# Routed experts in an alternating order, four table marks in flight, down remainders one item later, and the last rows prepared sooner

## The chip, the cores and the metric

The kernel runs on one core of one Trainium2 chip. The metric is the device time of one execution in microseconds (us). TensorE multiplies matrices; VectorE, ScalarE and GpSimd work on rows; SyncE issues most of the transfers, and GpSimd the gathers, the scattered additions and the accumulating loads.

## The reference

One encoder layer on 1024 tokens of width 1024, in fp32:

```
xn  = rms_norm(x);  z = xn @ w_in
A   = spatial gating of gelu(z[:, :1024]);  B = real part of a 2-D DFT of z[:, 1024:]
h   = x + concat(rms_norm(A), rms_norm(B)) @ w_out
hn  = rms_norm(h)
eidx, gates = top 8 of 64 experts for each token (sigmoid scores, best 4 of 8 groups)
routed[t]  = sum over the 8: gates * (silu(hn @ w_gate[e]) * (hn @ w_up[e])) @ w_down[e]
out = rms_norm(h + routed + shared expert)
```

An expert has a hidden width of 256. Its tokens are padded to a multiple of 128. The order in which the experts are done changes nothing but the rounding of sums.

## The kernel before, in words

The first part (projection, gating, DFT, w_out, router scores; lines 322 to 638) is not touched. Each token's expert set lies in `mask`.

**Routing tables** (lines 1249 to 1321 on VectorE, 667 to 703 on TensorE). TensorE counts the tokens of each expert by a product with ones. VectorE turns counts into numbers of 128-row pieces (`nch`), TensorE makes their running sum over the experts (line 686), VectorE derives from it `cols`: for item number p the expert (row 0 of `tab`) and twice the expert plus a bit for "first item of its expert" (row 1). Line 690 turns `cols` into rows, line 1296 writes `tab`, from which all engines read their registers (`look`). Then, chunk by chunk of 128 tokens, VectorE makes `mark` and `pick` (lines 1304, 1306) and TensorE multiplies them (`table`, line 663); the sum in `ps[5]` becomes `idx_all` and `row_all`, the token rows of every item. `mark` and `pick` have two places each, so chunk c waits for the product of chunk c - 2. Between these steps TensorE computes the shared expert (`s_gate_up`, `s_down`), and VectorE its `shared_h`.

**Items.** An item is 128 rows of one expert. Items come in turns of three (`TURN`), and a loop runs over the turns; the first and the last turn are written out. The experts are taken in the order of their numbers. An expert with more than 128 tokens has two items. For item i:
- GpSimd gathers its rows, three items ahead (`gather`), keeps the gate column (`keep_gate`, line 1527), and adds the result rows into DRAM (`add_rows`, line 1543), into one of two copies of y.
- TensorE runs, per step: the transposes of item i+1 (`turn_item`, line 460), `down(i - 1)` (line 733), `turn_h(i)` (line 741), `gate_up(i + 1)` (line 719). Every fp32 product is made of three in a faster format: high by high, high by rest, rest by high.
- ScalarE runs silu(i), `evac_xT(i + 1)`, the high half of the gate weights of item i+2 if that item starts an expert (`split_gu`, line 944), `evac_h(i)`, `evac_out(i - 1)`, the high half of the up weights, and then `split_dn` of item i+1's expert (line 948).
- VectorE runs `gated_h(i)` (hh, line 1329), `rest_xT(i + 1)` (xTl, 1336), the remainder of the gate weights for item i+2 (`rest_gu` part 0, line 1188), `rest_h(i)` (hTl, 1341), part 1, and `rest_dn` of item i+1's expert (1195).
- SyncE loads gate and up weights (1 MB each, lines 284 and 285) and down weights (1 MB, line 288) into two places each. A load waits until both halves of the expert two before are made (`load_next_gu`, `load_next_dn`).

TensorE's `down(i)` waits for the down weights (`s_hd`, `s_ld`) and for hTl (`s_hl`), and `gate_up(i)` for its weights (`s_hg`, `s_lg`) and xTl (`s_xd`).

**The end.** The rows of the last three items are not added in DRAM: GpSimd makes three one-hot matrices (`onehot`, line 1593), TensorE multiplies them with the last results (`last_rows`, 771), and VectorE adds the product to y (`add_last`, 1417). y is loaded by SyncE (line 448), and the second copy by accumulating loads of GpSimd (line 1601). `onehot` lies in `raw_dn`'s memory, so GpSimd and SyncE wait for the last `rest_dn` (lines 439 to 442 and 1587 to 1590).

The parts of VectorE's item that the change moves:

```
rest_xT(i + 1)
with dv.If(ahead[0] > 0): rest_gu(ahead[2], ahead[1], (0,))
rest_h(i)
with dv.If(ahead[0] > 0): rest_gu(ahead[2], ahead[1], (1,))
with dv.If(coming[0] > 0): rest_dn(coming[2], coming[1])
```

## Time and profile before

| | us |
|---|---|
| median of 3 runs | 1400.49 (1398.68 to 1400.86) |
| the profiled execution | 1402.79 |
| its span in the trace | 1401.1 |
| TensorE busy | 1327.6 (95%) |
| VectorE busy | 860.0 (61%) |
| ScalarE busy | 726.3 (52%) |
| GpSimd busy | 477.6 (34%) |
| HBM, mean over the span | 253 GB/s |

Times in rows are us from the start of the span. A row of the order of time has start, duration, engine, line, operation, written and read tiles, and in brackets the idle time of its engine before it and what ended that. Lines are those of the kernel before.

### The profile page before, as it was taken

Reading aid. Unit: us, or ns where it says so; the run is one execution under the profiler, and the core shown is the slowest. Engines: PE = TensorE matmul, PEld = TensorE weight load, DVE = VectorE, ACT = ScalarE, POOL = GpSimd, SP = SyncE. Lnnn points to the kernel's source line nnn. Section 1 sums busy time; section 2 is a strip of 40 time slices with the busy share of each in tenths; the row PEclk is TensorE's granted clock in tenths of the full one; section 3 lists DMA queues with packets and bytes.
Section 4 is the critical chain, followed back from the end, with each engine's and each line's share of the span. In section 5 each row is a group of like instructions: output and inputs, shape, how many; then the busy total and the mean of one; then the engine's idle time right before and its main releaser. Section 6 shows DMA issues by size and latency. Waiting matters only on the chain.

```text
span 1401.1 us, 25069 instructions
## 1 busy us (share of the span) xinstructions
PE 1327.6 (95%) x6025; PEld 1036.9 (74%) x6026; DVE 860.0 (61%) x1186; ACT 726.3 (52%) x916; POOL 477.6 (34%) x610
## 2 busy tenths in 40 slices
PE   6999988999999999999999999999999999999995
PEld 5885465888445888888878888878877788788774
DVE  5430543446565667667866566786687756675665
ACT  5321244221011576756865557675577756665752
POOL 2431201000001345435543334453354433433462
PEclk9999998999999999999999999999999999999998
DMA  9604022102306799999998889999899998998979
GB/s 347 181 6 161 5 115 91 46 31 102 131 16 233 251 307 329 341 294 317 336 369 264 247 264 297 375 351 276 262 350 372 354 268 264 323 317 273 301 240 242
DMA packets 88306, 338.01 MB, mean 241 GB/s; under 512 B 12497, under 2 KB 23761, under 8 KB 71505
## 3 DMA queue, kind: packets, MB, share of 16 engines
q1 hardware_dynamic: 60624, 250.53, 46.0%
q0 software_dynamic: 27648, 87.06, 27.5%
q8 instruction: 18, 0.29, 0.1%
q14 instruction: 16, 0.12, 0.0%
HBM read 288.99 MB, written 65.27 MB: 253 GB/s over the span
## 4 chain that ended last, share of the span: by engine, by line
PE 73%; DMA 9%; ACT 6%; DVE 4%; issue 4%; ACTq 2%; DVEq 1%; SPq 0%; POOL 0%; POOLq 0%
PE ps L719 28%; PE ps_out L733 11%; PE ps L611 6%; PE ps L477 6%; DMA raw_gu<-in_w_up 5%; PE ps L460 5%; PE ps L646 4%; PE ps L513 4%; ACT w_gu L944 3%; DMA ya_in<-y_rows_dram 2%; PE ps L562 2%; ACT w_dn L948 2%; DVE xTl L1336 1%; DMA raw_dn<-in_w_down 1%; PE ps_out L628 1%
## 5 line engine op out<-in xcount | busy, mean ns | idle before, releaser
L719 PE MATMUL ps<-w_gu,xTh 128*128 x1488 | 473.2, 399 | 21.6 <-DVE xTl L1336 20.6
L1188 DVE TENSOR_TENSOR w_gu<-raw_gu,w_gu (+1 forms) x128 | 293.5, 2293 | 106.8 <-ACT w_gu L944 106.3
L719 PEld LDWEIGHTS ps<-w_gu,xTh 128*128 128x128 f32 x1488 | 276.6, 190 | 84.6 <-issue 29.3
L719 PE MATMUL ps<-w_gu,xTl 128*128 x744 | 293.6, 395 | 0.0
L944 ACT ACTIVATE w_gu<-raw_gu (+1 forms) x128 | 245.6, 1920 | 17.8 <-SPq L396 17.7
L1543 POOL DMA_INDIRECT y_rows_dram<-ob,idxs x90 | 178.0, 1978 | 201.0 <-ACT ob L965 187.1
L733 PE MATMUL ps_out<-w_dn,hTh 128*128 x744 | 242.1, 407 | 1.6 <-ACT ob L965 1.6
L1195 DVE TENSOR_TENSOR w_dn<-raw_dn,w_dn (+1 forms) x128 | 150.9, 1220 | 69.0 <-ACT w_dn L948 69.0
L719 PEld LDWEIGHTS ps<-w_gu,xTl 128*128 128x128 f32 x744 | 141.3, 190 | 29.0
L1336 DVE TENSOR_TENSOR xTl<-ps,xTh 128x512 fp32r<-128x512 f32 x186 | 119.6, 685 | 55.2 <-ACT xTh L959 55.2
L733 PEld LDWEIGHTS ps_out<-w_dn,hTh 128*128 128x128 f32 x744 | 133.2, 189 | 26.9 <-issue 1.9
L733 PE MATMUL ps_out<-w_dn,hTl 128*128 x372 | 146.0, 392 | 0.0
L959 ACT ACTIVATE xTh<-ps 128x512 fp32r<-128x512 f32 x186 | 101.1, 595 | 79.3 <-PE ps L460 79.3
L948 ACT ACTIVATE w_dn<-raw_dn (+1 forms) x128 | 128.6, 1062 | 18.9 <-SPq L400 18.7
L1517 POOL DMA_INDIRECT Xg<-hn_rows_dram,idxg x94 | 102.7, 1092 | 76.8 <-POOL idxg L1514 74.7
L954 ACT ACTIVATE hs<-ps 128x256 f32<-128x256 f32 x93 | 35.6, 383 | 171.6 <-PE ps L719 170.5
L1527 POOL COPY gate<-Xg 128x1 f32 x93 | 35.6, 382 | 250.3 <-DVE hh L1329 145.6
L460 PEld LDWEIGHTS ps<-ident,Xg 128*128 128x128 f32 x744 | 96.8, 190 | 8.2 <-issue 0.7
L1465 POOL TENSOR_SCALAR rs<-ms 128x1 f32<-128x1 f32 x40 | 20.2, 505 | 235.3 <-ACT junk L814 234.2
L460 PE MATMUL ps<-ident,Xg 128*128 128x128 f32 x744 | 97.3, 274 | 0.0
L965 ACT ACTIVATE ob<-ps_out 128x1024 f32<-128x1024 f32 x92 | 94.3, 1025 | 0.0
L733 PEld LDWEIGHTS ps_out<-w_dn,hTl 128*128 128x128 f32 x372 | 69.9, 188 | 16.5
(213 smaller groups left out, 1581.2 us busy)
## 6 DMA issues: line engine op xcount, KB each, us to landing
raw_gu<-in_w_gate SPq DMA_DIRECT2D x64, 1024.0 KB, 7.0
raw_gu<-in_w_up SPq DMA_DIRECT2D x64, 1024.0 KB, 9.8
raw_dn<-in_w_down SPq DMA_DIRECT2D x64, 1024.0 KB, 12.7
y_rows_dram<-zero SPq DMA_DIRECT2D x1, 4608.0 KB, 20.0
x_ring<-in_x SPq DMA_DIRECT2D x8, 512.0 KB, 4.6
w_in_sb<-in_w_in SPq DMA_DIRECT2D x8, 512.0 KB, 9.7
xh<-in_x SPq DMA_DIRECT2D x8, 512.0 KB, 7.1
w_out_sb<-in_w_out SPq DMA_DIRECT2D x1, 4096.0 KB, 12.8
```

Source lines behind the costliest of these rows:

```text
L460: last = pe.transpose(ps[banks[k // 4]][:, (k % 4) * P:(k % 4 + 1) * P], src[:, k:D:KD], ident[:, :])
L719: mm = pe.matmul(ps[3][:, :], x_[:, k, :], w_gu[:, bass.ds(at, 1), part, :, k, :], start=(k == 0 and part == 0 and x_ is xTh), stop=(k == ...
L733: mm = pe.matmul(ps[6 + half][:, :], h_[:, k, :], w_dn[:, bass.ds(at, 1), part, k, half * 512:(half + 1) * 512], start=(k == 0 and part == ...
L944: act.activation(gu_part(w_gu[:, :, 0, :, :, :], at, m), gu_part(raw_gu, at, m), ACT.Copy).then_inc(s_hg, 1)
L948: act.activation(w_dn[:, bass.ds(at, 1), 0, k, :], raw_dn[:, bass.ds(at, 1), k, :], ACT.Copy).then_inc(s_hd, 1)
L959: act.activation(xTh[:, half * 4:half * 4 + 4, :], ps[1 + half][:, :].rearrange("p (k t) -> p k t", k=4), ACT.Copy).then_inc(s_xa, 1)
L965: act.activation(ob[:, u, :], ps_out[:, :], ACT.Copy).then_inc(s_oa, 1)
L1188: dv.tensor_tensor(gu_part(w_gu[:, :, 1, :, :, :], at, m), gu_part(raw_gu, at, m), gu_part(w_gu[:, :, 0, :, :, :], at, m).bitcast(F32), AL ...
L1195: dv.tensor_tensor(w_dn[:, bass.ds(at, 1), 1, k, :], raw_dn[:, bass.ds(at, 1), k, :], w_dn[:, bass.ds(at, 1), 0, k, :].bitcast(F32), ALU.s ...
L1336: dv.tensor_tensor(xTl[:, part, :], ps[1 + half][:, :].rearrange("p (k t) -> p k t", k=4), xTh[:, part, :].bitcast(F32), ALU.subtract).the ...
L1517: gp.indirect_dma_start(out=Xg[:, u, :], out_offset=None, in_=hn_d[:, :], in_offset=bass.IndirectOffsetOnAxis(ap=idxg[:, u:u + 1], axis=0) ...
L1543: gp.indirect_dma_start(out=y_d[:, :], out_offset=bass.IndirectOffsetOnAxis(ap=idxs[:, u:u + 1], axis=0), in_=ob[:, u, :], in_offset=None, ...
```

## The change

1. The experts get a new order. TensorE and VectorE compute a key for each expert from whether it has more than 128 tokens: the m-th of the experts with more gets m times the number of the others, plus 0.25; the m-th of the others gets (m + 0.5) times the number of the first kind. `upto` compares keys. The running sum of pieces goes by key, `tab` row 0 and 1 hold places in that order, and a third row gives the expert number at each place. SyncE and GpSimd look it up.
2. The first two experts' loads wait for `tab`.
3. `mark` has four places (in `w_dn`'s memory), `pick` four as well; chunk c waits for chunk c - 4. TensorE takes table 0 before, and tables 1 to 3 after `s_gate_up(2, 1)`.
4. `shared_h(3)` goes ahead of the index steps; the first transposes come after five `s_down` instead of four.
5. VectorE's `rest_dn` is done for the expert of item i (`now`) instead of item i+1, between `rest_xT` and `rest_gu`, and `rest_h` comes after both parts of `rest_gu`.
6. `onehot` moves to the memory of the gathered rows. Rows 0 and 1 are made before the gate of the last item is kept, row 2 after it. The loads of y no longer wait for `rest_dn`.

```diff
+            sp.wait_ge(s_tab, 1)
+            for j in range(2):
+                e = look(sp, 2, j, NE - 1)
+                load_gu(sp, e, 1 - j)
+                load_dn(sp, e, 1 - j)
...
-                load_gu(sp, e, at)
+                load_gu(sp, look(sp, 2, j, NE - 1), at)
...
-            sp.wait_ge(s_hd, NE * KF)
-            sp.sem_inc(s_turn_sp, 1)
-            sp.wait_ge(s_ld, NE * KF)
-            sp.sem_inc(s_turn_sp, 1)
...
+            pe.wait_ge(s_kinds, 1)
+            pe.matmul(ps[6][:, 0:NE], multi[:, :], tri[0:NE, 0:NE], start=True, stop=True)
+            pe.matmul(ps[6][:, NE:2 * NE], multi[:, :], identb[:, :], start=True, stop=True)
+            pe.matmul(ps[6][:, 2 * NE:2 * NE + 1], multi[:, :], ones[0:NE, 0:1], start=True, stop=True).then_inc(s_pm, 1)
+            s_gate_up(1, 0)
+
             pe.wait_ge(s_chunks, 1)
-            pe.matmul(ps[6][:, 0:NE], nchb[:, :], triI[:, :], start=True, stop=True).then_inc(s_pm, 1)
-            s_gate_up(1, 0)
+            pe.matmul(ps[7][:, 0:NE], nchb[:, :], upto[:, :], start=True, stop=True)
+            pe.matmul(ps[7][:, NE:2 * NE], nchb[:, :], identb[:, :], start=True, stop=True)
+            pe.matmul(ps[7][:, 2 * NE:3 * NE], ones[0:NE, :], upto[:, :], start=True, stop=True)
+            pe.matmul(ps[7][:, 3 * NE:3 * NE + 1], nchb[:, :], ones[0:NE, 0:1], start=True, stop=True).then_inc(s_pm, 1)
+            s_gate_up(1, 1)
...
+            step(dv.tensor_scalar(multi[:, :], ps[5][0:NE, 0:1].to_broadcast([NE, P]), float(P), None, ALU.is_gt))
+            dv.sem_inc(s_kinds, 1)
...
+            many((dv.tensor_scalar(key_t[:, 0, :], key_t[:, 0, :], 0.5, n_multi, ALU.add, ALU.mult),
+                  dv.tensor_scalar(key_t[:, 1, :], before, n_single, None, ALU.mult)))
...
+            step(dv.tensor_scalar(upto[:, :], key_t[:, 0, :], kinds[:, 3:4], None, ALU.is_ge))
...
-                if c >= 2:
-                    dv.wait_ge(s_table, c - 1)
+                if c >= 4:
+                    dv.wait_ge(s_table, c - 3)
...
                 rest_xT(i + 1)
                 if isinstance(i, int) and i == 0:
                     dv.wait_ge(s_yst[1], 16 * 4)
+                else:
+                    with dv.If(now[0] > 0):
+                        rest_dn(now[2], now[1])
                 with dv.If(ahead[0] > 0):
-                    rest_gu(ahead[2], ahead[1], (0,))
+                    rest_gu(ahead[2], ahead[1], range(GU_PARTS))
                 rest_h(i)
-                with dv.If(ahead[0] > 0):
-                    rest_gu(ahead[2], ahead[1], (1,))
-                with dv.If(coming[0] > 0):
-                    rest_dn(coming[2], coming[1])
...
             keep_gate(first + 1, 1)
             add_rows(two_less * TURN + (TURN - 1), TURN - 1, two_less)
+            gathers = turns(gp)
+            gp.wait_ge(s_ga[0], gathers * 16 + 16)
+            rows_of(0)
+            rows_of(1)
             keep_gate(first + 2, 2)
+            rows_of(2)
```

## Rows read from the trace of the kernel before

**Rows 1.** The page: busy time, share and instructions of each engine.

```profile
PE 1327.6 (95%) x6025; PEld 1036.9 (74%) x6026; DVE 860.0 (61%) x1186; ACT 726.3 (52%) x916; POOL 477.6 (34%) x610
```

**Rows 2.** The page: groups of ScalarE (count, busy, mean, idle before and releaser).

```profile
L954 ACT ACTIVATE hs<-ps 128x256 f32<-128x256 f32 x93 | 35.6, 383 | 171.6 <-PE ps L719 170.5
...
L944 ACT ACTIVATE w_gu<-raw_gu (+1 forms) x128 | 245.6, 1920 | 17.8 <-SPq L396 17.7
```

**Rows 3.** Busy time by stretches: length, busy us and count, PEclk, DMA share, GB/s.

```profile
560.00:700.00 140.00, 136.95 (x664) 112.95 (x663) 100.86 (x100) 97.31 (x114) 63.20 (x73) 1.00 0.98 322
...
740.00:860.00 120.00, 120.00 (x585) 99.74 (x585) 72.16 (x75) 70.25 (x89) 43.73 (x63) 1.00 0.87 259
...
1030.00:1110.00 80.00, 73.62 (x336) 59.54 (x337) 61.74 (x57) 56.48 (x63) 38.10 (x38) 0.96 1.03 374
```

**Rows 4.** VectorE in order of time: first, second and last hh.

```profile
450.18 0.48 DVE L1329 SCALAR_TENSOR_TENSOR hh<-hs,gate,ps 128x256 f32<-128x256 f32 x1 [2.36 <-ACT hs L954]
...
460.69 0.48 DVE L1329 SCALAR_TENSOR_TENSOR hh<-hs,gate,ps 128x256 f32<-128x256 f32 x1 [1.95 <-ACT hs L954]
...
1354.29 0.48 DVE L1329 SCALAR_TENSOR_TENSOR hh<-hs,gate,ps 128x256 f32<-128x256 f32 x1 [1.77 <-ACT hs L954]
```

**Rows 5.** TensorE in a pair: starts of two down products.

```profile
794.35 0.71 PE L733 MATMUL ps_out<-w_dn,hTh 128*128 x2
...
803.73 0.71 PE L733 MATMUL ps_out<-w_dn,hTh 128*128 x2
```

**Rows 6.** ScalarE in the same item: hTh and the second weight half.

```profile
797.65 0.38 ACT L969 ACTIVATE hTh<-ps 128x256 fp32r<-128x256 f32 x1
...
798.84 1.92 ACT L944 ACTIVATE w_gu<-raw_gu  x1
```

**Rows 7.** VectorE in the same item: xTl, hTl, second weight remainder.

```profile
795.26 1.29 DVE L1336 TENSOR_TENSOR xTl<-ps,xTh 128x512 fp32r<-128x512 f32 x2 [0.61 <-ACT xTh L959]
...
800.09 0.42 DVE L1341 TENSOR_TENSOR hTl<-ps,hTh 128x256 fp32r<-128x256 f32 x1
...
801.20 2.29 DVE L1188 TENSOR_TENSOR w_gu<-raw_gu,w_gu  x1 [0.69 <-ACT w_gu L944]
```

**Rows 8.** Passage from a pair to a one-item expert: TensorE and VectorE.

```profile
508.82 0.71 PE L733 MATMUL ps_out<-w_dn,hTh 128*128 x2
...
511.89 0.72 PE L719 MATMUL ps<-w_gu,xTh 128*128 x2
...
516.08 2.29 DVE L1188 TENSOR_TENSOR w_gu<-raw_gu,w_gu  x1 [0.44 <-ACT w_gu L944]
...
518.29 2.35 DVE L1195 TENSOR_TENSOR w_dn<-raw_dn,w_dn  x2
...
520.95 1.28 DVE L1336 TENSOR_TENSOR xTl<-ps,xTh 128x512 fp32r<-128x512 f32 x2
...
522.44 0.74 PE L719 MATMUL ps<-w_gu,xTh 128*128 x2 [0.89 <-DVE xTl L1336]
```

**Rows 9.** TensorE in the routing stage and at the first shared down product.

```profile
368.11 0.20 PE L686 MATMUL ps_out<-triI,nchb 64*128 64x64 bf16 x1
...
415.64 3.67 PE L656 MATMUL ps<-sd_w,hsT 128*128 128x512 f32 x8 [1.48 <-DVE hsT L1181]
```

**Rows 10.** The end: adds by rows, one-hot, loads of y, last addition.

```profile
L1543 POOL DMA_INDIRECT y_rows_dram<-ob,idxs x5: 1605/1792/3560, 1301.3 to 1340.4; - x5
...
DMA to landing us min/median/max: 6.4/8.0/9.4
...
1352.74 8.54 POOL L1593 TENSOR_SCALAR onehot<-tok_row,slot_col 128x1024 fp32r<-128x1024 f16 x3 [6.16 <-DVE w_dn L1195]
...
1353.72 3.85 SPq L448 DMA_DIRECT2D ya_in<-y_rows_dram  x8
...
1391.17 1.29 DVE L1417 TENSOR_TENSOR ya_in<-ps,ya_in 128x512 f32<-128x512 f32 x2 [1.36 <-DMA ya_in<-y_rows_dram]
```

**Rows 11.** GpSimd: a gate column beside a remainder of VectorE.

```profile
880.96 0.63 POOL L1527 COPY gate<-Xg 128x1 f32 x1 [0.20 <-issue]
```

More of the change, by code:

```diff
@@ L204, in build @@
         ya_in = place("ya_in", [P, NC, D], F32, U_AT)
-        onehot = place("onehot", [P, TURN, S], F32R, Z_AT)
+        onehot = [place(f"onehot{u}", [P, S], F32R, W_AT + 32 * KB + u * GATED * 4) for u in range(TURN)]
         ob_high = place("ob_high", [P, TURN, D], F32R, X_AT)
@@ L780, in _ @@
             pe.wait_ge(s_hm, 4)
-            for c in range(4):
+            for c in range(5):
                 s_down(c)
             turn_item(0, 1)
-            for c in range(4, NC):
+            for c in range(5, NC):
                 s_down(c)
@@ L1317, in _ @@
                     shared_h(2)
+            shared_h(3)
             dv.wait_ge(s_table, NC)
@@ L1321, in _ @@
             dv.tensor_tensor(row_all[:, :], idx_all[:, :], copy_row[:, :], ALU.add).then_inc(s_idx, 1)
-            shared_h(3)
             def gated_h(i, u):
@@ L1348, in expert, with item @@
                 return dv.snap(both % 2, min_val=0, max_val=1), e, place_of(dv, e)
-            def item(i, u, coming, final=False):
+            def item(i, u, now, coming, final=False):
                 gated_h(i, u)
@@ L1364, in item @@
                     dv.wait_ge(s_yst[1], 16 * 4)
+                else:
+                    with dv.If(now[0] > 0):
+                        rest_dn(now[2], now[1])
                 with dv.If(ahead[0] > 0):
[L1366 removed]
+                    rest_gu(ahead[2], ahead[1], range(GU_PARTS))
                 rest_h(i)
[L1368 to L1371 removed]
                 return ahead
             def turn_of_items(turn, final=False):
[L1375 removed]
+                now, coming = expert(turn * TURN), expert(turn * TURN + 1)
                 for u in range(TURN):
[L1377 removed]
+                    now, coming = coming, item(turn * TURN + u, u, now, coming, final and u > 0)
             def y0(c):
```

105 lines of the change are left out of this document (59 added, 46 removed).

## The prediction

> **What bounds the kernel now.** I read the page, then the busy time by stretches, then the order of time on each engine inside single items. The page gives TensorE 95% busy, before all others [rows 1]. There are 93 items (one silu each) and 64 experts (two gate and up halves each, 128) [rows 2]; no expert has more than two items in the trace, so 29 experts have two (first item A, second item B) and 35 have one (item S). From the first hh to the last the item phase takes 1354.29 - 450.18 = 904.11 us, 92 intervals, 9.83 on average [rows 4]. In the stretch of nothing but A B pairs TensorE never pauses (120.00 of 120.00 us); where one-item experts follow each other it is busy 73.62 of 80 and the DMA engines are full [rows 3]. From one down product to the next in a pair is 803.73 - 794.35 = 9.38 us [rows 5]: that is the floor of an item. 10.51 (the first interval, which a cold start sets) + 91 x 9.38 = 864.1, so 40 us of the phase lie above the floor.
>
> Where they lie is seen at a passage from a pair to a one-item expert. Item B there must do the weight remainders of the next expert but one (two of 2.29) and of the next expert's down matrix (two, 2.27 us) [rows 8]. VectorE does both behind B's rest_h, so the next hh and xTl come late, and gate_up starts at 522.44 where the item before started it at 511.89: 10.55, which is 1.17 over the floor [rows 8]. 29 A B S cycles at that price would be 34 us. Alternation alone therefore only spreads the loss; it is the move of rest_dn that could take it away.
>
> **The change, part by part.**
>
> *The order.* With 29 pairs and 35 singles the keys give A B S 29 times, and 6 extra S. The item count, the bytes and the products stay.
>
> *rest_dn one item later.* In item i VectorE now does hh(i), xTl(i+1), rest_dn(i) if i starts an expert, both parts of rest_gu(i+2) if i+2 starts one, and only then rest_h(i). A does everything, B only rest_gu, S (before an A) only rest_dn; two full items never follow each other, and the sum of VectorE's work is unchanged. TensorE's down(i) waits for rest_h(i) too, and comes straight after the products of item i+1. I work with D, the start of the down product in the item, 794.35 [rows 5]. xTl is over at 795.26 + 1.29, D+2.20 [rows 7]; rest_dn adds 2.27 (D+4.5), the first part of rest_gu 2.21 (D+6.7). The second part waits for ScalarE, which starts its half after hTh and ob, at D+4.49 [rows 6], and VectorE begins it at 801.20, D+6.85 [rows 7]. So rest_dn fits into a gap that exists: its cost is nothing, covered by ScalarE's half; without that cover it would be 2.27. The second part takes 2.21 to the next instruction [rows 8], rest_h starts at D+9.06 and ends at +0.42 [rows 7], D+9.48. From an xTl that ends at 520.95 + 1.28 to its product is 0.21 us [rows 8]; I take the same from hTl to down: D+9.69. The floor wants it at D+9.38. **What is late next is hTl**: 0.31 per A. For B ScalarE is later, rest_gu's second part starting at 516.08, 7.26 after the product at 508.82 [rows 8]. A wait of 0.31 just ahead makes that 6.95, and 6.95 + 2.21 + 0.42 + 0.21 = 9.79, or 0.41 over. The six S that are followed by another S are full items too: 0.31. Sum: 29 x 0.31 + 29 x 0.41 + 6 x 0.31 = 22.7. The phase becomes 864.1 + 22.7 = 886.8, **17.3 less**. This wait is not in the trace of before (there rest_h sits between the two parts), so its bounds are: nothing, if down overlaps it, and a whole 0.88 more per full item, if each of the two branches shows the 0.44 that VectorE needs behind ScalarE's half (798.84 + 1.92 to 801.20) [rows 6, 7]. The middle is nearest to rows of the same instructions.
>
> *Loads.* load_dn of an expert is now released in item A or S at D+4.5 instead of at the end of the item before. An A B S cycle leaves two items for 1 MB. Where two S meet, the next A's down weights get some 11 us from issue to use; I put nothing there, since the halves made from them are needed an item later still, and 1 us at each of the 6 as an upper bound. An expert is three loads of 1024 KB, 3.15 MB; the pairs' 259 GB/s over 18.85 us are 4.88 MB, so an item's own rows are 0.87. The even order wants (64 x 3.15 + 93 x 0.87) MB / 887 us = 319 GB/s; 322 stand in the trace with a DMA share of 0.98 and TensorE 136.95 of 140 busy, and 374 with 1.03 [rows 3]: enough, with little to spare.
>
> *The first loads* leave at the tables instead of after the last w_out product. 6 MB at the 374 GB/s of [rows 3] are 17 us, from about 384 to 401, and ScalarE comes to them behind the shared expert's last silu, about 414 [rows 9]: hidden; with no cover it would be 17 us once.
>
> *The routing stage.* TensorE is busy there with the shared expert. One small product took 0.20 us there [rows 9]. Six more of them, three at a new stop and three at the old one, are 1.2 at most; they overlap each other, and I take 0.8. VectorE's some 17 new short steps run while TensorE does gate_up products of 7 us; four marks in flight keep the fourth chunk off TensorE's path. shared_h(3) ahead of the table wait takes the two index steps out of the 1.48 for which the first shared down product waits [rows 9]; I take 0.5 of it. Net +0.3, bounds -0.7 and +1.5.
>
> *The end.* The last accumulating loads are what the end waits for: the DMA engines are full from 1353.72, where the plain loads of y leave, to the last add at 1391.17 [rows 10]. They left when the last rest_dn was done. Now they wait for rest_gu (over 9 us earlier) and the adds of item 89: issued at 1340.39, landing after 8.0 (6.4 to 9.4), so at 1348.4 plus 0.3 [rows 10]. **5.0 us earlier** (3.6 to 6.6). The one-hot rows (8.54 us, from 1352.74) go to GpSimd's idle time before the last item; the accumulating loads then need not wait for them.
>
> GpSimd reading beside VectorE is slow in the trace: a one-column gate copy took 0.63 at 880.96 beside a running rest_dn [rows 11]. I charge the rows nothing, since the gate of the last item is due 12 us after they can start, and they need 8.54 for all three [rows 10]. The Trainium skill ("SBUF — State Buffer", Who interferes with whom) says that a VectorE instruction with two SBUF inputs and a GpSimd one that reads SBUF exclude each other, and that the later one is blocked for the whole instruction. The gate copy agrees. By that rule a one-hot row that comes first would hold up a remainder by up to its own 2.85 (8.54 / 3), and the sum would be up to 2.9 us worse.
>
> **Sum** against the profiled execution (1402.79, span 1401.1; 2.3 above the median of the runs): +0.3 - 17.3 - 5.0 = -22.0. I take the same off the median: 1400.49 - 22.0 = **1378.5 us**.
>
> **Rivals.**
> 1. *No wait for hTl.* Every item at the floor: 40.0 + 5.0 - 0.3 = 44.7 less, 1355.8. For it: the floor is held for 120 us on end, and the wait is a few tenths. Against: the order in rest_h's new place, and that ScalarE's half is bound to TensorE's own progress, so it cannot run ahead.
> 2. *Branches exposed.* In a full item the two branches before rest_dn and rest_gu cost 0.44 each; 0.2 of it falls into the gap, the rest delays rest_h: 35 x 0.62 = 21.7. 1378.5 + 21.7 = 1400.2, no change. Against: between separate branches the remainders follow each other without a gap (516.08 + 2.21 = 518.29) [rows 8].
> 3. *Late loads, slower.* The place is ScalarE's wait for gate and up weights. Where the DMA share is 1.03, TensorE is busy 73.62 of 80 us [rows 3], which makes an item of 9.38 one of 10.19; if each of the 62 loads in the loop costs that 0.81, the phase is 864.1 + 50.2 = 914.3 and the whole 1400.49 + 0.3 + 10.2 - 5.0 = 1406.0. It decides from 0.72 us per load on (44.7 / 62). For it: the share of 0.98 at the rate wanted. Against: an alternating order gives a load three items instead of two.
> 4. *The order buys all, the move nothing* (the passage keeps its 1.17): 35 x 1.17 = 41 over the floor, as before, and only the end gains: 1400.49 - 5.0 + 0.3 + 1 = 1396.8.
>
> **How the numbers follow.** Forecast 0.47, rival 1 0.23, rival 2 0.10, rival 3 0.10, rival 4 0.10. A difference of 0.2% (2.8 us) is about what measurements of this kernel tell from none. Forecast, rival 1 and rival 4 are faster, with a little of rival 2: 0.82; rival 2 otherwise, 0.07; rival 3 and the worse side of rival 2, 0.11. The range 1355 to 1398 takes in rival 1, the bounds of the hTl wait and rival 4, and leaves out most of 2 and 3.
>
> **What would show it.** Right: intervals between hh near 9.7 on average in an A B S cycle; TensorE waits at the down line released by hTl, 0.3 to 0.4 us, some 60 times; no more waits of gate_up for xTl of 0.9; the plain y loads 6 us before the last hh instead of 0.6. Wrong: intervals of 9.38 (rival 1); gaps between xTl and rest_dn (2); ScalarE's w_gu waits for SyncE far over their 17.7 us [rows 2] (3); gate_up still waiting for xTl (4).

## The result and the profile after

The changed kernel takes 1410.35 us (median of 4 runs, 1409.56 to 1412.08) beside 1400.67 for the kernel before (1398.68 to 1401.01). The ratio is 1.0066 [1.0049, 1.0083]: slower by 0.7%, where 1378.5 and "faster" had been forecast, and outside the range. The profiled execution has a span of 1409.2 us against 1401.1.

Three stretches make up the 8.1 us of difference: up to the first hh 2.5 less, from the first hh to the last 920.4 against 904.11 us [rows 4], so 16.3 **more**, and from the last hh to the end of the span 41.1 against 46.8, so 5.7 less. The whole surprise is in the item phase, for which 17.3 less had been forecast.

The page of the kernel after, its line of engines, and the group of ScalarE's weight halves (columns as in [rows 2]):

```profile
PE 1325.5 (94%) x6030; PEld 1035.9 (74%) x6032; DVE 857.3 (61%) x1203; ACT 727.0 (52%) x916; POOL 467.1 (33%) x610
...
L955 ACT ACTIVATE w_gu<-raw_gu (+1 forms) x128 | 245.6, 1919 | 42.8 <-SPq L404 37.5
```

No engine has more work to speak of than before [rows 1]. ScalarE's wait for SyncE has gone from 17.7 [rows 2] to 37.5 us. L1363 is hh now, L744 down, L730 gate_up, L1375 hTl, L955 the gate and up halves, L1199 their remainders.

The row of hh (first and last start), and busy time in the stretches of [rows 3]:

```profile
L1363 DVE SCALAR_TENSOR_TENSOR hh<-hs,gate,ps x93: 461/472/481, 447.7 to 1368.1; 128x256 f32<-128x256 f32 x93
```

```profile
560.00:700.00 140.00, 133.48 (x644) 110.17 (x643) 95.49 (x95) 93.32 (x110) 57.70 (x70) 1.00 0.95 309
740.00:860.00 120.00, 114.07 (x550) 94.06 (x549) 83.67 (x83) 79.60 (x94) 48.47 (x61) 1.00 0.94 304
1030.00:1110.00 80.00, 76.60 (x371) 63.16 (x369) 54.64 (x54) 53.55 (x64) 33.10 (x41) 1.00 0.92 293
```

All stretches look alike now, as an alternating order should make them. But TensorE is 95 to 96% busy in each (133.48 of 140, 114.07 of 120, 76.60 of 80), and the DMA share is 0.92 to 0.95 at 293 to 309 GB/s, less than the 0.98 and 322, and the 1.03 and 374, that [rows 3] show. So the DMA engines have room.

The waits of the item phase (who waited for whom, us in total, times, longest):

```profile
ACT w_gu L955 <- SPq L404: 37.5, 30, 2.3
PE ps_out L744 <- DVE hTl L1375: 36.3, 36, 1.4
...
PE ps L730 <- DVE xTl L1370: 2.7, 3, 1.7
```

The same for SyncE itself, which waits for a landing before it tells ScalarE of it:

```profile
SPq L404 <- DMA raw_gu<-in_w_up: 9.6, 5, 6.3
```

The wait of gate_up for xTl, 20.6 us in 26 places before, is gone as forecast. In its place down waits for hTl, as forecast too, but for up to 1.4 us, not 0.3 to 0.4. And the transfers aren't what ScalarE waits for: SyncE had to wait for a landing of gate and up weights in 5 places, 9.6 us in all (before 38.5 in 19), while ScalarE waited for SyncE's word in 30.

**One cycle.** VectorE, SyncE, ScalarE and TensorE of the kernel after in order of time, from item A through B to S and the next A:

```profile
737.43 0.48 DVE L1363 SCALAR_TENSOR_TENSOR hh<-hs,gate,ps 128x256 f32<-128x256 f32 x1 [5.05 <-ACT hs L965]
...
737.61 0.71 PE L744 MATMUL ps_out<-w_dn,hTh 128*128 x2
...
741.99 4.59 DVE L1199 TENSOR_TENSOR w_gu<-raw_gu,w_gu  x2
...
746.83 0.47 DVE L1363 SCALAR_TENSOR_TENSOR hh<-hs,gate,ps 128x256 f32<-128x256 f32 x1
...
747.33 0.73 PE L744 MATMUL ps_out<-w_dn,hTh 128*128 x2
...
748.68 0.34 SPq L291 DMA_DIRECT2D raw_gu<-in_w_gate  x1
...
749.93 1.92 ACT L955 ACTIVATE w_gu<-raw_gu  x1 [1.03 <-SPq L404]
...
757.66 0.47 DVE L1363 SCALAR_TENSOR_TENSOR hh<-hs,gate,ps 128x256 f32<-128x256 f32 x1
...
758.17 0.72 PE L744 MATMUL ps_out<-w_dn,hTh 128*128 x2 [1.20 <-DVE hTl L1375]
...
767.38 0.48 DVE L1363 SCALAR_TENSOR_TENSOR hh<-hs,gate,ps 128x256 f32<-128x256 f32 x1 [5.05 <-ACT hs L965]
...
767.56 0.71 PE L744 MATMUL ps_out<-w_dn,hTh 128*128 x2
```

The forecast counts from one down product to the next. A takes 747.33 - 737.61 = 9.72, B 758.17 - 747.33 = 10.84, S 767.56 - 758.17 = 9.39. A and S are what the forecast gave (9.69 and 9.38). B is at 10.84 where 9.79 was forecast: about one microsecond too much, 29 times. (From one hh to the next the same cycle reads A to B 9.40, B to S 10.83, S to A 9.72; the experiments are told in these.) Read backwards: TensorE waits 1.20 for hTl, which stands behind both remainders, which wait for ScalarE's halves, and ScalarE began its first half at 749.93, after 1.03 of waiting for a signal of SyncE (L404, the increment that says "the gate and up weights have landed"). In SyncE's program that signal stands **behind the next load**. The load waits for VectorE's remainder of A, over at 741.99 + 4.59 = 746.58, and then SyncE looks up which expert to load; its first transfer is issued at 748.68, 2.10 us later. The read of the table in that lookup, first this one, then all those of the item phase (shortest, median and longest in ns):

```profile
L318 SPq TENSOR_LOAD <-tab x1: 1440/1440/1440, 746.8 to 746.8; - x1
```

```profile
L318 SPq TENSOR_LOAD <-tab x123: 5/276/1510, 456.1 to 1343.0; - x123
```

The remainder, the load and ScalarE's half in the kernel before, VectorE, SyncE, ScalarE:

```profile
506.29 2.29 DVE L1188 TENSOR_TENSOR w_gu<-raw_gu,w_gu  x1 [0.69 <-ACT w_gu L944]
...
508.83 0.34 SPq L284 DMA_DIRECT2D raw_gu<-in_w_gate  x1
...
510.74 1.92 ACT L944 ACTIVATE w_gu<-raw_gu  x1
```

There the remainder ends at 508.58 and the load goes out 0.25 us later. The lookup, `look(sp, 2, j, NE - 1)`, evaluated between the waits and the load, costs 2.10 - 0.25 = 1.85 us here, and everything behind it on SyncE is late by that. It isn't one price. Behind item A of a cycle the load goes out 2.05 to 2.34 us behind the remainder in 24 cases and 3.92 to 4.39 in three; behind the other items it is 0.91 to 1.84, at the least 0.66 more than before. At A the read itself is the slow part (1.44 us against a median of 0.28). ScalarE and VectorE read the same table beside it, in 0.99 and 1.36 us; that the three hold each other up is likely from this, but no run shows it.

### The profile page after: what moved, and what is told of

The parts are those of the page before. It is cut to its first block, busy times and chain, and to the rows that moved or that the text cites. A ratio compares the mean times of both kernels' runs of the same rounds, so it can differ in the third digit from the quotient of the medians.

```text
span 1409.2 us, 25989 instructions
## 1 busy us (share of the span) xinstructions
PE 1325.5 (94%) x6030; PEld 1035.9 (74%) x6032; DVE 857.3 (61%) x1203; ACT 727.0 (52%) x916; POOL 467.1 (33%) x610
## 4 chain that ended last, share of the span: by engine, by line
PE 47%; ACT 12%; DVE 11%; issue 10%; DMA 7%; SPq 7%; DVEq 3%; ACTq 2%; POOL 0%; POOLq 0%
PE ps L730 11%; DVE w_gu L1199 9%; ACT w_gu L955 8%; PE ps L481 6%; PE ps L615 6%; PE ps_out L744 5%; PE ps L650 4%; PE ps L517 4%; DMA raw_dn<-in_w_down 4%; SPq L318 4%; PE ps L464 2%; DMA ya_in<-y_rows_dram 2%; PE ps L566 2%; DVEq L318 2%; ACT ob L976 1%
## 5 line engine op out<-in xcount | busy, mean ns | idle before, releaser
L730 PE MATMUL ps<-w_gu,xTh 128*128 x1488 | 468.9, 396 | 2.7 <-DVE xTl L1370 2.7
L1199 DVE TENSOR_TENSOR w_gu<-raw_gu,w_gu (+1 forms) x128 | 292.5, 2290 | 88.3 <-ACT w_gu L955 87.9
L730 PEld LDWEIGHTS ps<-w_gu,xTh 128*128 128x128 f32 x1488 | 273.3, 189 | 57.4 <-issue 4.1
L730 PE MATMUL ps<-w_gu,xTl 128*128 x744 | 292.0, 393 | 0.0
L1578 POOL DMA_INDIRECT y_rows_dram<-ob,idxs x90 | 191.6, 2129 | 273.7 <-ACT ob L976 266.1
L744 PE MATMUL ps_out<-w_dn,hTh 128*128 x744 | 242.9, 408 | 40.1 <-DVE hTl L1375 36.3
L955 ACT ACTIVATE w_gu<-raw_gu (+1 forms) x128 | 245.6, 1919 | 42.8 <-SPq L404 37.5
L744 PEld LDWEIGHTS ps_out<-w_dn,hTh 128*128 128x128 f32 x744 | 133.9, 188 | 77.0 <-issue 51.9
L730 PEld LDWEIGHTS ps<-w_gu,xTl 128*128 128x128 f32 x744 | 140.0, 188 | 29.5
L744 PE MATMUL ps_out<-w_dn,hTl 128*128 x372 | 146.1, 393 | 0.0
L1363 DVE SCALAR_TENSOR_TENSOR hh<-hs,gate,ps 128x256 f32<-128x256 f32 x93 | 44.1, 474 | 150.1 <-ACT hs L965 150.1
L1562 POOL COPY gate<-Xg 128x1 f32 x93 | 17.8, 191 | 205.0 <-DVE hh L1363 115.2
## 6 DMA issues: line engine op xcount, KB each, us to landing
w_in_sb<-in_w_in SPq DMA_DIRECT2D x8, 512.0 KB, 10.2
```

The source lines that it names most:

```text
L730: mm = pe.matmul(ps[3][:, :], x_[:, k, :], w_gu[:, bass.ds(at, 1), part, :, k, :], start=(k == 0 and part == 0 and x_ is xTh), stop=(k == ...
L744: mm = pe.matmul(ps[6 + half][:, :], h_[:, k, :], w_dn[:, bass.ds(at, 1), part, k, half * 512:(half + 1) * 512], start=(k == 0 and part == ...
L955: act.activation(gu_part(w_gu[:, :, 0, :, :, :], at, m), gu_part(raw_gu, at, m), ACT.Copy).then_inc(s_hg, 1)
L1199: dv.tensor_tensor(gu_part(w_gu[:, :, 1, :, :, :], at, m), gu_part(raw_gu, at, m), gu_part(w_gu[:, :, 0, :, :, :], at, m).bitcast(F32), AL ...
L1578: gp.indirect_dma_start(out=y_d[:, :], out_offset=bass.IndirectOffsetOnAxis(ap=idxs[:, u:u + 1], axis=0), in_=ob[:, u, :], in_offset=None, ...
```

## The experiments

All ran beside the kernel before, whose median was 1401.2 to 1402.5 in the five sets of runs; a gain is read from the ratio. "Phase" is first hh to last hh.

**1. The lookup ahead of the waits** (look_early: the change, with this):

```diff
 def load_next_gu(j, at):
+    e = look(sp, 2, j, NE - 1)
     sp.wait_ge(s_hg, (j - 1) * GU_PARTS)
...
-    load_gu(sp, look(sp, 2, j, NE - 1), at)
+    load_gu(sp, e, at)
```

(and the same in `load_next_dn`.)

> The changed kernel, but SyncE reads the expert number of the next load ahead of its waits instead of behind them. Theory 1 (the register lookup stands between VectorE's last gate and up remainder and the landing signal that SyncE gives ScalarE for the expert before, and so holds up ScalarE's halves in item B by about 0.9 us): B's interval falls from 10.75 to about 9.85, the item phase from 920.4 to about 893, the time to about 1383. Theory 2 (the weights themselves land late, from bandwidth): no change, 1410. In both, hTl still holds up the down product in A and B.

Measured: 1381.41 us (1380.63 to 1382.4), ratio 0.9859 [0.9833, 0.9885], phase 890.1. Its waits, and B and S in the order of time:

```profile
ACT w_dn L961 <- SPq L410: 49.9, 23, 4.9
...
PE ps_out L746 <- DVE hTl L1377: 2.9, 5, 0.6
...
ACT w_gu L957 <- SPq L406: 0.3, 1, 0.3
```

```profile
737.65 0.47 DVE L1365 SCALAR_TENSOR_TENSOR hh<-hs,gate,ps 128x256 f32<-128x256 f32 x1
...
739.65 1.92 ACT L957 ACTIVATE w_gu<-raw_gu  x1
...
747.39 0.47 DVE L1365 SCALAR_TENSOR_TENSOR hh<-hs,gate,ps 128x256 f32<-128x256 f32 x1
```

ScalarE's half starts 2.00 behind hh of B instead of 749.93 - 746.83 = 3.10; its wait for the signal has gone from 37.5 to 0.3 us, and B takes 9.74. Theory 1 had given 893 and 1383. GpSimd's second lookup, in `keep_gate`, is still there and so isn't the cause. Four lines of one queue's program are worth 28.9 us, and what is left is within 3 us of the forecast's 1378.5. That this is so near is partly luck: the first interval takes 8.88 where 10.51 was charged, and where two S meet the next intervals are 10.84, 11.24, 11.79 and 12.25 at four of the six places, where some 9.7 were expected.

**2. Twice the lookup** (look_twice: the change, and a second, unused `look(sp, 2, j, NE - 1)` in the gate and up load).

> The changed kernel with a second register lookup of the same kind ahead of each pair of gate and up loads. Theory 1: B's interval grows by one more lookup, about 1.8 us, the phase by 29 x 1.8 plus the six places of two S, 50 to 60 us; the time near 1465. Theory 2: no change, since the loads have many us to spare against bandwidth.

Measured: one run, 1428.63 us; phase 937.8, 17.4 more than with one lookup. ScalarE's wait for the signal goes from 37.5 to 48.0 us; B takes 11.33 (hh at 750.78 and 762.11), 0.5 more and not 1.8. The direction is confirmed, the size missed by far more than half. The trace says why: of the two reads in a row at A the first takes 1.4 to 1.5 us and the second 0.27, and the load goes out some 0.7 us later than with one lookup. The second read isn't cheaper than others; the first one is dear in that place.

**3 and 4. rest_h back between the parts** (hTl_between: the change with this; both: with this and the early lookup). It takes away the 0.31 to 0.41 that the forecast charged.

```diff
-    rest_gu(ahead[2], ahead[1], range(GU_PARTS))
+    rest_gu(ahead[2], ahead[1], (0,))
 rest_h(i)
+with dv.If(ahead[0] > 0):
+    rest_gu(ahead[2], ahead[1], (1,))
```

> The changed kernel with hTl back between the two remainders of gate and up weights; rest_dn stays one item later and the lookup stays where it is. Theory 1 with the hTl wait: the down product no longer waits for hTl; ScalarE's late halves in B make hh of S late by 1 us, which the slack in front of gate_up takes. All intervals near 9.4, the phase near 866, the time near 1356. If late landings (theory 2) or VectorE's total work bound the phase, B's interval stays above 10.3 and the time above 1395.

> The lookup ahead of the waits and hTl between the remainders. Theory 1: no better than hTl between alone, 1354 to 1357, since the late halves already cost nothing there. If the two costs add up independently (0.9 and 0.3 to 0.4 per item), it is 27 us faster than hTl between alone.

Measured: hTl_between 1382.08 us (1379.83 to 1386.61), ratio 0.9868 [0.9835, 0.9902]; both 1387.07 (1383.12 to 1388.99), 0.9889 [0.986, 0.9919]. Two misses: neither is near 1356, and the second is no better than look_early. But hTl_between tells as much as look_early: with the **late** lookup left in, moving rest_h alone takes off 28.3 us. ScalarE's half in B is as late as in the change (hh at 737.27, the half at 740.51 after 1.18 of waiting for SyncE), and so is hh of S (748.06, 10.79 behind); the next hh comes 8.16 later, and the three intervals from B on (10.79, 8.16, 9.39) make 28.34, as the theory's slack had it. So the late signal costs TensorE time in the change because hTl stands behind the remainders that wait for it. With rest_h between them the early lookup gains nothing (the ratios 0.9868 and 0.9889 lie inside each other's intervals). Both stay far from 1356, and another wait has grown. A row of the waits of both (hTl_between has 76.1 us in 24 places there), and SyncE and ScalarE in the order of time (hh of B at 739.14, of S at 748.28):

```profile
ACT w_dn L961 <- SPq L410: 106.1, 28, 7.0
```

```profile
739.47 0.34 SPq L291 DMA_DIRECT2D raw_gu<-in_w_gate  x1
...
742.02 0.19 SPq L295 DMA_DIRECT2D raw_dn<-in_w_down  x1
...
756.91 2.01 ACT L961 ACTIVATE w_dn<-raw_dn  x2 [4.15 <-SPq L410]
```

The larger expert's down weights are asked for at 742.02, behind 2 MB of gate and up weights, and ScalarE can start only some 15 us later, after waiting for 4.15. Their place had been free since 734.5 (its remainder is done in item A); the load stood behind the gate and up load, which waits for a later remainder.

**5 and 6. A first other list for SyncE** (sp_order: on both; after_sp_order: on the change itself), each load as soon as its predecessor landed:

```diff
 with sp.Fori(1, NE // 2 - 1) as t:
-    load_next_gu(t * 2 + 1, 0)
     gu_landed(1, t + 1)
     load_next_dn(t * 2, 1)
-    dn_landed(0, t)
+    load_next_gu(t * 2 + 1, 0)
+    dn_landed(1, t + 1)
```

(the second half of the loop and the lines behind it likewise.)

> The kernel 'both' (lookup ahead of the waits, hTl between the remainders) with SyncE's list rearranged: for each expert x the landing signal of its gate and up weights, the load of its down weights, the load of the next expert's gate and up weights, the landing signal of its down weights. Theory 3 (in 'both' ScalarE's down halves in S wait until 8 to 10 us because A's down weights are loaded only behind the next expert's gate and up weights, and are signalled only behind a load that waits for S's rest_dn): the halves start near 4.7, all intervals near 9.4, phase near 868, time near 1358. If instead the DMA engines are simply full at this rate, the down halves stay late and the time stays above 1378.

> The changed kernel with SyncE's list rearranged in the same way, and nothing else: the lookup still stands behind the waits, hTl still comes last. Theory 1 in its wider form (it is the signal standing behind the lookup and load that costs, not the lookup as such): as good as the early lookup or a little better, B's interval near 9.7, time 1376 to 1383. If the lookup itself costs wherever it stands: 1410.

Measured: 1412.9 us (1408.53 to 1417.46), ratio 1.0079 [1.0059, 1.01]; and 1430.9 (1429.28 to 1432.64), 1.0208 [1.0192, 1.0224]. Both clear misses. SyncE's own waits in sp_order:

```profile
SPq L406 <- DMA raw_gu<-in_w_up: 384.9, 56, 8.4
SPq L410 <- DMA raw_dn<-in_w_down: 217.6, 60, 5.9
```

In both they are 47.2 and 87.7. SyncE now stands 600 us waiting for landings, among them that of a load it has itself just issued, and meanwhile it can issue nothing. A landing wait too early in the list does as much harm here as a signal too late.

**7 and 8. The parts of the change one by one** (order_only_dn_old: the new order, lookup and end, but `rest_dn` and `rest_h` where they were; before_dn_between: the kernel before with `rest_dn` one item later, `rest_h` left between the parts).

```diff
 rest_xT(i + 1)
+with dv.If(now[0] > 0):
+    rest_dn(now[2], now[1])
...
-with dv.If(coming[0] > 0):
-    rest_dn(coming[2], coming[1])
```

(before_dn_between; order_only_dn_old is the change with these lines the other way round and `rest_gu` in two parts.)

> The changed kernel with rest_dn back at the end of VectorE's item (for the expert of item i+1), and hTl between the parts as before: the alternating order without the move. Forecast's view (the passage costs 1.17 at each of 29 places when the halves are on time) plus the late signal (0.9): passages cost about 2, phase 864 + 60 = 924, time near 1413. If alternation alone pays by balance, it is below 1395.

> The kernel before (experts by number, loads by constants of the loop, no lookup) with rest_dn one item later and hTl still between the two parts. By the forecast's arithmetic the passages from a pair to a single (1.17 each, about 15 of them) and the runs of singles lose their VectorE part: about 20 us faster than before, 1380, if SyncE's landing signals stay on time. If the chain of SyncE's waits bites here too (the down signal behind a load that waits for the later rest_dn), it is 1395 or worse.

Measured: order_only_dn_old 1413.7 us (1412.12 to 1417.02), ratio 1.0091 [1.0073, 1.0109]; before_dn_between 1401.18 (1399.63 to 1405.18, 10 runs), 1.0003 [0.9992, 1.0015]. The move of rest_dn alone, in the old order, does nothing. One of its waits:

```profile
ACT w_dn L948 <- SPq L400: 61.0, 23, 6.5
```

(18.7 us in 9 places before the change; ScalarE's wait for gate and up weights grows too, from 17.7 to 37.4. So the second branch of the expectation came true: what the move takes from VectorE comes back as waits for SyncE.)

**9 and 10. The order with an early lookup, and the end alone** (dn_old_look_early: order_only_dn_old with the lookup ahead of the waits; tail_only: the kernel before with the one-hot rows in their new memory, made ahead of the last gate, and SyncE's two waits removed).

> The new order and the new end, rest_dn where it was (behind both parts of rest_gu, for item i+1) and rest_h between the parts, and SyncE's lookup ahead of its waits. It tells what the move of rest_dn is worth once the lookup no longer delays a signal. Theory (the signal in B is 0.95 us late because of the lookup, and the passage out of B costs 1.17 over the floor of 9.38 where rest_dn stands behind B's rest_gu): against the same kernel with the late lookup (1413.7) about 29 x 0.95 = 28 less by the signal, so 1386 +- 5, and the move (1381.4 with the early lookup) is worth only some 5 us. Rival (the move pays as the forecast said, 35 x 1.17 minus its hTl waits, 17): 1398 or more.

> The kernel before with the change's end alone (one-hot rows in the memory of the gathered rows, made ahead of the last gate; loads of y not behind rest_dn). Theory: the forecast's 5.0 us from the end stand by themselves, 1396 +- 1. Rival: the gain belongs to the new order of the last experts, and before keeps its 1401.

Measured: dn_old_look_early 1391.71 us (1391.1 to 1393.69), ratio 0.9929 [0.9908, 0.9951], a little above its band, and so the move, rest_h's included, is worth 10.3 where some 5 had been expected; tail_only 1394.54 (1392.14 to 1397.03), 0.9944 [0.9925, 0.9963], its last hh at the same 1354.3 as before. So the end is worth 8 us alone (7.2 in the span), and the order alone on top of it 1394.5 - 1391.7, some 3, which the two intervals don't tell from nothing.

The runs in the new order give two choices side by side, how VectorE's item is arranged and where the lookup stands:

| VectorE's item | lookup behind the waits | ahead of them |
|---|---|---|
| rest_dn in its old place, rest_h between the parts | 1413.7 (order_only_dn_old) | 1391.7 (dn_old_look_early) |
| rest_dn one item later, rest_h between the parts | 1382.1 (hTl_between) | 1387.1 (both) |
| rest_dn one item later, rest_h behind both parts | 1410.35 (the change) | 1381.4 (look_early) |

The late lookup costs 22.0, nothing, and 28.9 us. Moving rest_dn with rest_h left where it was is worth 31.6 us with the late lookup and 4.6 with the early one, the latter hardly clear of noise. Moving rest_h behind both parts costs 28.3 with the late lookup and nothing with the early one. None of the three has a price of its own; each depends on what stands behind what.

**11 and 12. A list by due times** (due_order: on look_early; both_due: on both). Each load stands where its place comes free in an A B S cycle, each signal just ahead of its use; 2t is the larger expert:

```diff
 with sp.Fori(1, NE // 2 - 1) as t:
-    load_next_gu(t * 2 + 1, 0)
     gu_landed(1, t + 1)
     load_next_dn(t * 2, 1)
     dn_landed(0, t)
+    load_next_gu(t * 2 + 1, 0)
     load_next_gu(t * 2 + 2, 1)
-    gu_landed(0, t + 1)
+    dn_landed(1, t + 1)
     load_next_dn(t * 2 + 1, 0)
-    dn_landed(1, t + 1)
+    gu_landed(0, t + 1)
```

> The early lookup (1381.4) and a new order of SyncE's program, by when each place comes free in an A B S cycle: signal gu(2t), load dn(2t), signal dn(2t-1), load gu(2t+1), load gu(2t+2), signal dn(2t), load dn(2t+1), signal gu(2t+1). Theory: in B ScalarE's half starts at h+1.4 instead of h+1.9, because its signal no longer stands behind the load that waits for A's rest_gu; hTl in B is then not 9.4 but 9.1 behind hh, and each cycle saves 0.3 us, 9 in all: 1372 (1370 to 1377). Rival (the landing waits come too early in the list and hold up later loads, as in the list tried before): over 1385. Rival 2 (ScalarE's own order sets it): no change, 1381.

> The same list on the kernel with the early lookup and rest_h back between the parts (1387.1 with the old list, where the split of the down weights in S waits some 100 us in all for SyncE). Theory (A's down weights come late because load dn(2t) stands behind load gu(2t+1), whose place comes free 4.6 us later): the wait for SyncE in front of the down half falls under 20 us, every item of a cycle comes to the floor of 9.38, 1358 (1355 to 1366). Rival (the transfers themselves are late, the DMA engines being full): the wait stays over 60 us and the time stays over 1380.

Measured: due_order 1413.23 us (1411.15 to 1414.54), ratio 1.0077 [1.0053, 1.01]; both_due 1385.05 (1381.47 to 1385.53), 0.987 [0.9846, 0.9895]. Misses again, by far on look_early, where ScalarE's half in B starts 3.2 us behind hh in the same items as below. But both_due is not the same everywhere. Three hh in a row from both_due, an item A, B and S:

```profile
548.30 0.48 DVE L1365 SCALAR_TENSOR_TENSOR hh<-hs,gate,ps 128x256 f32<-128x256 f32 x1 [3.80 <-ACT hs L967]
557.70 0.48 DVE L1365 SCALAR_TENSOR_TENSOR hh<-hs,gate,ps 128x256 f32<-128x256 f32 x1
568.56 0.47 DVE L1365 SCALAR_TENSOR_TENSOR hh<-hs,gate,ps 128x256 f32<-128x256 f32 x1
```

B costs 10.86 here, and 10.87 to 11.52 in the cycles up to item 23. Before that stretch intervals are 9.4 to 9.6 (the first apart), up to the place where two S meet, which takes 14.48; behind it they are 8.8 to 9.7. Two smaller experts meet at items 8 and 9 and put every larger one behind them on an odd place until two more meet at 24 and 25, and the list is written for even ones. The same happens twice more (13.83 and 13.31 where two S meet, then B at 10.7 to 11.4). Three B of 10.2 in a stretch with even places (items 62 to 68) aren't explained by it.

**13 to 15. A strict order**, larger, smaller, 29 times, and the six smaller ones that are left at the end (both_due_strict, both_strict and look_early_strict, on both_due, both and look_early). Both factors of the key become 1:

```diff
-many((dv.tensor_scalar(n_multi, ps[6][0:NE, 2 * NE:2 * NE + 1], 1.0, None, ALU.max),
+many((dv.tensor_scalar(n_multi, ps[6][0:NE, 2 * NE:2 * NE + 1], 1.0, 1.0, ALU.max, ALU.min),
...
-step(dv.tensor_scalar(n_single, kinds[:, 2:3], 1.0, None, ALU.max))
+step(dv.tensor_scalar(n_single, kinds[:, 2:3], 1.0, 1.0, ALU.max, ALU.min))
```

> Early lookup, rest_h between the parts, SyncE's list by due times, and the order of experts strict: larger, smaller, larger, smaller for 58 experts and the six smaller ones that are left over at the end (both key factors set to 1). In the run with the same list and the spread order, intervals of 9.37 to 9.38 stand where larger experts have even places (items 29 to 31), and 10.9 per cycle is lost at item B where a single smaller one has shifted them to odd places (items 11 to 23), as the list is written for even ones. Theory (the list fits even places alone): 29 cycles at the floor of 3 x 9.38; the last six at what the DMA engines give, 4.02 MB per item at 374 GB/s, 10.75 each, 8 us lost: 1356 + 8 = 1364 (1360 to 1370). Rival (the floor of a whole cycle can't be held, since the transfers are late): 1378 or more.

> As the last, with SyncE's old list. Theory (the down weights of the larger expert stand behind the gate and up load of the smaller one, whose place comes free later, in whichever order the experts come): no better than 1387, the wait of ScalarE's down half for SyncE stays near 100 us. Rival (the extra smaller experts alone do the harm): 1364 too.

> The change with the early lookup alone and the strict order. It has rest_h behind both parts of rest_gu, so each cycle costs 9.41 + 9.71 + 9.70 and not 3 x 9.38. Theory: 29 x (28.82 - 28.14) = 20 over the floor, and 8 for the six at the end: 1384 +- 4, the list mattering little here. Rival (the six spread ones cost more than the six at the end): under 1378.

Measured: 1383.83 us (1381.2 to 1384.65), ratio 0.9869 [0.9845, 0.9893]; 1385.36 (1383.59 to 1389.46), 0.9889 [0.9861, 0.9918]; 1379.05 (1378.61 to 1380.18), 0.9842 [0.982, 0.9863]. ScalarE's wait for the down weights, first both_strict, then both_due_strict:

```profile
ACT w_dn L961 <- SPq L410: 106.8, 30, 4.9
```

```profile
ACT w_dn L961 <- SPq L410: 1.1, 1, 1.1
```

With the same bytes in the same order of experts, the list alone takes 105.7 us off that wait. Yet the two totals are nearly the same, because of the last six. hh of both_due_strict there, and a row of ScalarE between them:

```profile
1263.82 0.48 DVE L1365 SCALAR_TENSOR_TENSOR hh<-hs,gate,ps 128x256 f32<-128x256 f32 x1
...
1270.18 1.92 ACT L957 ACTIVATE w_gu<-raw_gu  x1 [4.04 <-SPq L406]
...
1278.38 0.48 DVE L1365 SCALAR_TENSOR_TENSOR hh<-hs,gate,ps 128x256 f32<-128x256 f32 x1 [0.46 <-POOL gate L1566]
1287.75 0.47 DVE L1365 SCALAR_TENSOR_TENSOR hh<-hs,gate,ps 128x256 f32<-128x256 f32 x1
1304.94 0.47 DVE L1365 SCALAR_TENSOR_TENSOR hh<-hs,gate,ps 128x256 f32<-128x256 f32 x1
```

Up to item 86, at 1263.82, it is 9.2 us ahead of look_early_strict (1273.0), and then items take 14.56, 9.37 and 17.19: where smaller experts follow each other, the signals stand in the wrong place. So the total of 1364 was missed, and the cycle nearly met: 28.4 us each up to item 86 against 3 x 9.38 = 28.14. The rival's 1378 or more came true for another reason, in the last six. look_early_strict, at 1379.05, is 1 us under its band and above its rival's; against look_early (0.9859) its ratio is within the intervals, so six smaller experts at the end and six spread ones cost the same as far as these runs tell.

**16. Each list where it fits** (due_then_old: both_due_strict, with the due list for t = 1 to 28 and the old one for the rest). The number 29 is that of these inputs, so this is a measurement, not a kernel for any routing.

```diff
-with sp.Fori(1, NE // 2 - 1) as t:
+with sp.Fori(1, 29) as t:
...
+with sp.Fori(29, NE // 2 - 1) as t:
...
```

> both_due_strict with its list by due times only where larger and smaller experts alternate (the first 58), and the old list for the six smaller ones at the end. both_due_strict holds 28.4 us per cycle up to item 86 (hh at 1263.8) and loses 14.6 to 17.7 us in items 87 to 91, where no place comes free in the order of the list; the strict order with the old list (look_early_strict) needs 63.8 us from item 86 to the last. Theory (the list is all there is to it): last hh at 1263.8 + 63.8 = 1327.6 instead of 1336.8 in look_early_strict (1379.05), so 1370 (1367 to 1373). Rival (rest_h between the parts is what makes the end slow, as in both_strict's intervals of 10.4 to 13.0): 1374 or more. Rival 2 (the waiting loads only moved the transfers' debt to the end): 1379 or more.

Measured: **1370.41 us** (1369.43 to 1371.53), ratio 0.9779 [0.9764, 0.9794], last hh at 1325.8: the theory's 1370, with the last hh 1.8 earlier than its 1327.6. It is the fastest of all, 2.2% below the kernel before and 2.8% below the change. A cycle of it, and busy time in the first and last stretch of [rows 3]:

```profile
730.85 0.48 DVE L1374 SCALAR_TENSOR_TENSOR hh<-hs,gate,ps 128x256 f32<-128x256 f32 x1 [3.78 <-ACT hs L976]
740.22 0.48 DVE L1374 SCALAR_TENSOR_TENSOR hh<-hs,gate,ps 128x256 f32<-128x256 f32 x1
749.78 0.48 DVE L1374 SCALAR_TENSOR_TENSOR hh<-hs,gate,ps 128x256 f32<-128x256 f32 x1
759.35 0.48 DVE L1374 SCALAR_TENSOR_TENSOR hh<-hs,gate,ps 128x256 f32<-128x256 f32 x1 [3.80 <-ACT hs L976]
```

```profile
560.00:700.00 140.00, 139.99 (x679) 115.91 (x678) 98.82 (x100) 95.67 (x114) 61.20 (x75) 1.00 0.99 314
...
1030.00:1110.00 80.00, 80.00 (x390) 66.35 (x389) 56.43 (x57) 53.20 (x64) 35.54 (x41) 1.00 0.99 320
```

28.50 us per cycle against a floor of 3 x 9.38 = 28.14. TensorE hardly pauses (119.96 of 120 in the stretch not shown), and the bytes arrive at 314 to 320 GB/s with a share of 0.99. That TensorE's products themselves take 0.1 us per item more than the floor is seen and wasn't traced further.

## Why the prediction was wrong

*What bounds the kernel, the floor, the passage.* Right. 9.38 came back wherever nothing was late, and the wait of gate_up for xTl went from 20.6 to 2.7 us as it should with the move.

*The order and the move.* The claim that alternation alone only spreads the loss holds: some 3 us alone, not clear of noise. That the move could take the loss away was right with alternation, in part: 10.3 us with the early lookup, and 31.6 with the late one and rest_h left between the parts, but only 3.4 as the change has it (1413.7 to 1410.35), where the wait for hTl takes the rest. In the old order, with rest_h between the parts, rest_dn's move gave nothing (1.0003); the prediction says nothing on that case.

*The wait for hTl.* Right in place; right in size for A and S (9.72 and 9.39 against 9.69 and 9.38). For B it was wrong, 10.84 against 9.79, and look_early, where down products stand 9.75 apart in B, 9.39 in S and 9.77 in the next A, shows that 9.79 would have been right without the late lookup. TensorE's weight loads at the down line stand idle there 20.8 us in all, 63 times, where the forecast had 22.7 and some 60 (the trace names no releaser for most of them; down starts 0.35 to 0.45 behind hTl's end). What it would cost to be without this wait was wrong in rival 1: with rest_h between the parts and the early lookup (both) the time is 1387, not 1356, and ScalarE's wait for the down weights, 49.9 us in look_early, is 106.1.

*B's wait for hTl and the loads: the step that failed.* The term of the sum that was too small is the one for B: 0.41 us over the floor was charged and 10.84 - 9.38 = 1.46 measured, 1.05 too little at each of 29 places, some 30 us. It was read from a row of before, in which rest_gu's second part starts 7.26 behind the product [rows 8], as if ScalarE's halves would start in the new kernel when they start in the old one. They don't, because of the second half of the step: the part on loads counts bytes and rates, charges nothing, and names the lookup nowhere, though the diff puts a register read inside `load_next_gu` and `load_next_dn`, behind the waits and ahead of everything else SyncE does. At A it cost 1.85 us, and the signal for ScalarE's half in B stands behind it. The part speaks of when a load leaves, not of what is queued behind it on its engine, so the range had no room for that. Experiment 1 puts the missing term at 28.9 us, 30.3 in the phase (920.4 - 890.1); with it the sum would have been 1378.5 + 28.9 = 1407.4 against 1410.35. The term is one of two together, and not the lookup's alone: hTl_between keeps the lookup late and is 28.3 us faster than the change, since down no longer waits behind the late halves.

That the term has this sign could have been had from the two kernels' text and the trace of before: SyncE's list puts the load ahead of the signal, and ScalarE's half starts there 510.74 - 508.83 = 1.91 behind the load's issue, where 749.93 - 748.68 = 1.25 is what a half needs that waits for the signal alone. That is a slack of 0.66 against a delay of 1.85: by this estimate about 1.2 us exposed, 29 times; in fact the hh of B and ScalarE's half are 3.10 apart now, and 2.00 in look_early. The size was harder to have: in the trace of before, VectorE's reads of the same table take 0.34 us in the median of 121, and only the longest 1.55. By the same estimate a read at its least delay in the kernel after, 0.66, would just have been hidden.

*The rivals.* Rival 3 named the right place (ScalarE's wait for gate and up weights) and the right sign, 1406.0, by a mechanism that isn't there: the DMA engines were less full than before (0.92 to 0.95), and SyncE waited for landings of gate and up weights 9.6 us in all, not 38.5. That its 1406.0 is nearest of all is luck. Rival 2's exposed branches would add 0.62 per full item; look_early's cycle of 9.41, 9.74 and 9.72 has no room for them. Rival 4's passage of 1.17 isn't in that cycle either.

*First loads and the routing stage.* +0.3 was forecast. The first hh is 2.5 earlier, but 1.95 of that lies ahead of the routing stage, whose code is the same, so the stage gave 0.5: right within its bounds. tail_only and before_dn_between, which start like the kernel before, have their first hh at 448.30 and 448.29; the 1.9 is a difference between executions.

*The end.* 5.0 forecast, 5.7 in the trace, 8 with tail_only; right in mechanism, a little small. The loads of y, VectorE's last remainder and the third one-hot row in the kernel after:

```profile
1362.20 4.72 SPq L452 DMA_DIRECT2D ya_in<-y_rows_dram  x8
...
1364.85 2.36 DVE L1206 TENSOR_TENSOR w_dn<-raw_dn,w_dn  x2 [1.77 <-ACT w_dn L959]
...
1364.87 4.98 POOL L1620 TENSOR_SCALAR onehot<-tok_row,slot_col 128x1024 fp32r<-128x1024 f16 x1
```

And the second row and the last remainder in tail_only:

```profile
1349.20 2.85 POOL L1581 TENSOR_SCALAR onehot<-tok_row,slot_col 128x1024 fp32r<-128x1024 f16 x1
```

```profile
1350.30 2.36 DVE L1191 TENSOR_TENSOR w_dn<-raw_dn,w_dn  x2 [1.77 <-ACT w_dn L944]
```

The plain loads leave 5.93 before the last hh (1368.13), as said. The third one-hot row took 4.98 where the two before it took 2.88 and 2.85: it met VectorE's last remainder, which started 0.02 before it and runs 2.36. In tail_only the first row took 4.79, 0.22 behind the start of a remainder. This agrees with the exclusion of the Trainium skill ("SBUF — State Buffer", Who interferes with whom) where VectorE comes first. It does not bear out the case for which the prediction reckoned with up to 2.9, a row that comes first: in tail_only the remainder starts 1.10 behind the row, and both take their usual 2.36 and 2.85.

## What to carry to other kernels

Price every instruction that a change puts on a queue engine, and then ask what stands behind it in that engine's program: here a register read ahead of a signal came to 1.85 us in the place that mattered and, with hTl behind the work that waits for that signal, cost 29 us; moving it ahead of the waits turned a loss of 0.7% into a gain of 1.4%. Take its price from that place and not from its median (1.44 us against 0.28 here). An engine that waits, loads and signals from one list needs that list in the order in which places come free and signals fall due, and such a list fitted one pattern of work only in these runs: changing the order of the work meant writing the list anew. When a wait is taken away, look for the one it was covering before its whole length is counted as gain.

## What the runs showed of the hardware

- SyncE's read of a register from the on-chip table took 0.28 us in the median of 123, and 1.44 us at 746.8, while VectorE and ScalarE read the same table (1.36 and 0.99 us). With address computation and issue, the transfer went out 2.10 us behind the releasing instruction against 0.25 without a read; in other places 0.91 at the least. A second read right behind the slow one took 0.27 us (look_twice).
- GpSimd's 128x1024 one-hot row took 2.85 to 2.88 us, and 4.79 to 4.98 where a VectorE remainder of the down weights (raw_dn and w_dn in, w_dn out) had started just before it. Where the row had started first, row and remainder took their usual 2.85 and 2.36 (tail_only).
- The DMA engines show a share of 0.99 at 314 to 320 GB/s in one kernel and 1.03 at 374 in another stretch [rows 3]: a full share is not one rate.
